# Two transformer blocks in one fp32 kernel: fillers recounted, weights split in halves, and five edits at the seams between stages

## The reference

```python
mixed = einsum('bsgc,gcd->bsgd', pooled - xg, w)
h = mixed.reshape(B, S, D) * scale
...
def _swiglu(x, w_gate, w_up, w_down):
    return (silu(x @ w_gate) * (x @ w_up)) @ w_down
...
def squared_relu_mlp(xn, w_up, w_down):
    return jnp.square(jax.nn.relu(xn @ w_up)) @ w_down
```

## Time and profile before

| what | value |
|---|---|
| time, median of 3 runs | 998.71 us |
| the profiled execution's own time | 998.4 us |
| its span, first to last instruction | 996.2 us |
| TensorE matmul / weight load busy | 977.4 / 863.7 us |
| VectorE / ScalarE / GpSimd busy | 665.5 / 449.8 / 32.4 us |
| mean granted TensorE clock | 0.999 |
| chain that ended last | 88% TensorE |
| bytes moved by DMA | 176.2 MB, 177 GB/s |

### The profile page before, as it was taken

One profiled execution on the slowest core, in us unless ns is written; L12 is line 12 of the kernel. 1 busy time (PEld: TensorE's weight loads), 2 busy tenths in 40 slices (PEclk: granted clock), 3 DMA queues, 4 the chain that ended last, 5 costly groups with the idle time before them and its releaser, 6 DMA issues.

```text
span 996.2 us, 15345 instructions
## 1 busy us (share of the span) xinstructions
PE 977.4 (98%) x6071; PEld 863.7 (87%) x6071; DVE 665.5 (67%) x814; ACT 449.8 (45%) x562; POOL 32.4 (3%) x54
## 2 busy tenths in 40 slices
PE   8999999999999999999999999999999999999997
PEld 7888888888996888888889878899999888888886
DVE  3776767685776876666676477775876656666663
ACT  3444444445665253434334446565654443434342
POOL 1000001000001000000001000000000000000000
PEclk9999999999999999999999999999999999999999
DMA  9756677548532456656543644543565535656541
GB/s 307 233 185 228 190 238 220 193 147 226 157 128 85 148 192 231 206 194 195 184 146 136 193 143 127 158 128 127 170 212 178 194 135 171 207 176 207 170 168 43
DMA packets 142175, 176.20 MB, mean 177 GB/s; under 512 B 7040, under 2 KB 120898, under 8 KB 142126
## 3 DMA queue, kind: packets, MB, share of 16 engines
q1 hardware_dynamic: 139040, 167.07, 52.1%
q0 software_dynamic: 2464, 8.30, 2.8%
q10 hardware_dynamic: 622, 0.14, 0.1%
HBM read 174.40 MB, written 1.09 MB: 176 GB/s over the span
## 4 chain that ended last, share of the span: by engine, by line
PE 88%; DVE 5%; ACT 3%; issue 2%; DMA 1%; ACTq 1%; POOL 0%; DVEq 0%; POOLq 0%; SPq 0%
PE bank L499 87%; DVE w_lo L990 2%; ACT w_hi L982 1%; PE bank L634 1%; PE bank L742 1%; DMA raw<-w_up 1%; DVE arena L1430 1%; DVE x_both L1360 0%; POOL rstd L1885 0%; ACTq L1250 0%; ACT bank L1258 0%; DVE arena L1455 0%; DVE arena L1444 0%; ACT arena L1139 0%; ACTq L1253 0%
## 5 line engine op out<-in xcount | busy, mean ns | idle before, releaser
L990 DVE TENSOR_TENSOR w_lo<-raw,w_hi 128x2048 fp32r<-128x2048 f32 (+1 forms) x157 | 353.5, 2256 | 164.2 <-ACT w_hi L982 164.0
L499 PE MATMUL bank<-x_both,w_hi 128*128 128x256 f32 (+1 forms) x2128 | 439.3, 330 | 2.6 <-DVE arena L1430 1.4
L499 PEld LDWEIGHTS bank<-x_both,w_hi 128*128 128x128 f32 x2128 | 357.6, 189 | 44.3 <-issue 6.7
L982 ACT ACTIVATE w_hi<-raw 128x2048 fp32r<-128x2048 f32 (+1 forms) x157 | 294.9, 1881 | 109.6 <-PE bank L499 98.7
L499 PE MATMUL bank<-x_both,w_lo 128*128 128x256 f32 x1520 | 287.6, 283 | 0.4 <-DVE arena L1430 0.4
L499 PEld LDWEIGHTS bank<-x_both,w_lo 128*128 128x128 f32 x1520 | 230.2, 191 | 3.9 <-issue 0.6
L499 PE MATMUL bank<-w_hi,arena_r 128*128 128x512 f32 x608 | 172.5, 392 | 1.2 <-DVE arena_r L1463 1.0
L499 PEld LDWEIGHTS bank<-w_hi,arena_r 128*128 128x128 f32 x608 | 113.1, 188 | 25.6 <-issue 2.4
L499 PE MATMUL bank<-w_lo,arena_r 128*128 128x512 f32 x304 | 96.1, 391 | 0.0
L1430 DVE TENSOR_REDUCE arena<-bank 128x512 f32<-128x1024 f32 x57 | 69.7, 1222 | 24.8 <-PE bank L499 24.8
L499 PE MATMUL bank<-w_hi,x_both 128*128 128x512 f32 x256 | 75.0, 393 | 2.3 <-DVE x_both L1360 0.8
(11 more groups left out here) (155 smaller groups left out, 612.2 us busy)
## 6 DMA issues: line engine op xcount, KB each, us to landing
raw<-w_up SPq DMA_DIRECT2D x76, 512.0 KB, 4.6
raw<-w_down SPq DMA_DIRECT2D x76, 512.0 KB, 4.3
raw<-w_in SPq DMA_DIRECT2D x60, 512.0 KB, 4.5
raw<-w_gate SPq DMA_DIRECT2D x44, 512.0 KB, 4.8
raw<-w_qkv SPq DMA_DIRECT2D x24, 512.0 KB, 5.0
raw<-w_o SPq DMA_DIRECT2D x16, 512.0 KB, 4.4
table<-bias_vectors POOLq DMA_DIRECT2D x12, 256.0 KB, 4.9
raw<-w_pa SPq DMA_DIRECT2D x4, 512.0 KB, 4.2
```

The lines of the kernel that those rows point to most:

```text
L499: return nc.tensor.matmul(*a, skip_group_check=True, **k)
L982: last = nc.scalar.activation(o, i, ACT.Copy)
L990: last = nc.vector.tensor_tensor(o, i, h.bitcast(F32), ALU.subtract)
```

## The change

Seven edits:

1. **Fillers.** `keep_warm` counts change from 16, 6, 24, 30, 14, 16 to 12, 3, 13, 12, 12, 7 (norm 0, v norm, norm 3, ahead of norm 4, norm 4, norm 5), and the 5 at the end of each seam to 3. The 10 fillers of `warm` ahead of the mixing become 3.
2. **Start.** The 16 opening fillers become four fp32r products of 512 columns. `pool_scale` comes as one row of 4 KB on ScalarE's queue; TensorE spreads it by two products with a column of ones, VectorE copies them to `gb`. ScalarE's table load is drawn ahead by a tiny activation.
3. **Small products** come ahead of the mixing, and wait for all four copies of the pooled x (`pool_copied`) first.
4. **Halves.** ScalarE and VectorE split each unit in two halves of 1024 columns; `hi_done` counts halves.
5. **MLP chunk 1** uses the banks 6 and 7.
6. **Mixer norm.** VectorE multiplies by the gain alone (`with_gain`), ScalarE applies rstd (`scaled`) and raises `n_ready`; ScalarE's rounding of unit `U_QI + 1` goes behind the seam.
7. In the same norm the rests come in the order (0,0), (0,1), (1,0), (1,1), and the first projection waits for `x_ready` 3 and then 4 of the four, where it waited for 2 and 4.

```diff
-            eng.dma_start(gb[:, 2, :], t["pool_scale"].rearrange("a b -> (a b)").partition_broadcast(P))\
-                .then_inc(scale_in, 16)
...
-            keep_warm(bank[4], 5)
+            keep_warm(bank[4], 3)
...
         def pe_mlp(eng):
-            def up(i, unit, slot, final=False):
+            def up(i, unit, slot, final=False, fresh=False):
                 eng.wait_ge(lo_done, unit + 1)
+                if fresh:
+                    project_apart(slot, pair67).then_inc(unit_done, 1)
+                    return
                 eng.wait_ge(up2_read, i)
...
...
         @block.tensor
         def _(eng):
-            for n in range(4 * KT // 2):
-                c = n % 4 * P
-                last = mm(bank[n // 4][:, c:c + P], warm, warm, start=(c == 0), stop=True)
+            for n in range(4):
+                last = mm(bank[n][:, :], opener[:, 0:P], opener, start=True, stop=True)
             last.then_inc(psum_open, 1)
+            eng.wait_ge(set_done, 3)
+            for _ in range(4):
+                mm(bank[6][:, 0:P], warm, warm, start=True, stop=True)
+            eng.wait_ge(scale_in, 16)
+            for h in range(2):
+                mm(bank[4 + h][:, :], ones[0:1, :], scale_row[:, half(h)], start=True, stop=True)\
+                    .then_inc(scale_spread, 1)
+            for _ in range(3):
+                mm(bank[6][:, 0:P], warm, warm, start=True, stop=True)
+            eng.wait_ge(scale_copied, 2)
             eng.wait_ge(pool_m_in, 16)
...
-            for _ in range(10):
+            for _ in range(3):
                 mm(bank[4][:, 0:P], warm, warm, start=True, stop=True)
+            eng.wait_ge(pool_copied, NG)
+            eng.wait_ge(small_in, SMALL)
+            nc.tensor.transpose(bank[7][:, 0:NROWS], prow, ident[0:NROWS, 0:NROWS]).then_inc(pe_start, 1)
+            eng.wait_ge(set_done, 5)
+            mm(bank[7][0:24, 64:448], tab, onehot, start=True, stop=True).then_inc(pe_start, 1)
+            eng.wait_ge(lam_prod, 1)
+            mm(bank[7][:, 448:450], ones, lprod, start=True, stop=True).then_inc(pe_start, 1)
...
-            eng.wait_ge(small_in, SMALL)
-            nc.tensor.transpose(bank[7][:, 0:NROWS], prow, ident[0:NROWS, 0:NROWS]).then_inc(pe_start, 1)
...
             eng.wait_ge(small_read, 4)
-            pe_norm_end(eng, 0, x, 16, 0)
+            pe_norm_end(eng, 0, x, 12, 0)
...
-            pe_norm_end(eng, 3, x, 24, 3)
+            pe_norm_end(eng, 3, x, 13, 3)
             pe_ffn(eng, 1, 3)
-            keep_warm(bank[5], 30)
-            pe_norm_end(eng, 4, nbuf, 14, 4)
+            keep_warm(bank[5], 12)
+            pe_norm_end(eng, 4, nbuf, 12, 4)
...
-            pe_norm_end(eng, 5, nbuf, 16, 6)
+            pe_norm_end(eng, 5, nbuf, 7, 6)
...
         def round_unit(eng, unit, slot, landed, fresh=False, indexer=False):
...
+            for h in range(2):
+                c = slice(h * UW // 2, (h + 1) * UW // 2)
+                nc.scalar.activation(w_hi[slot][:, c], raw[slot][:, c], ACT.Copy).then_inc(hi_done, 1)
...
         def rest_unit(eng, unit, slot, indexer=False):
...
+            for h in range(0 if indexer else 2):
+                eng.wait_ge(hi_done, unit * 2 + (h + 1))
+                c = slice(h * UW // 2, (h + 1) * UW // 2)
+                last = nc.vector.tensor_tensor(w_lo[slot][:, c], raw[slot][:, c], w_hi[slot][:, c].bitcast(F32),
+                                               ALU.subtract)
             last.then_inc(lo_done, 1)
...
             s_ffn(eng, 1)
+            def scaled(i):
+                eng.wait_ge(rstd_ready, 11 + i)
+                for h in range(2):
+                    eng.wait_ge(zg_ready, 2 * i + h + 1)
+                    nc.scalar.activation(nbuf[:, i, half(h)], nbuf[:, i, half(h)], ACT.Identity,
+                                         scale=rstd[:, i:i + 1]).then_inc(n_ready, 1)
             s_rms(eng, 0, (0,))
-            s_split(eng, U_QI + 1)
+            scaled(0)
             s_rms(eng, 0, (1,))
-            s_rounds(eng, 4)
+            s_rounds(eng, 4, (0,))
+            scaled(1)
+            s_rounds(eng, 4, (1,))
+            s_split(eng, U_QI + 1)
...
             v_ffn(eng, 1)
...
+            def with_gain(i, h):
+                V.tensor_tensor(nbuf[:, i, half(h)], x[:, i, half(h)], gb[:, 2, half(h)], ALU.mult)\
+                    .then_inc(zg_ready, 1)
...
-            v_rms_rows(eng, 0, n_rms, 2, False)
...
-            v_rms_rows(eng, 1, n_rms, 2, False)
```

More of the change, by code:

```diff
@@ L313, in build @@
         scale_in = sem("scale_in")
+        scale_spread = sem("scale_spread")
+        scale_copied = sem("scale_copied")
         ln0_in = sem("ln0_in")
@@ L537, in first_apart @@
             whi, wlo = (part(w, unit % SLOTS, KT) for w in (w_hi, w_lo))
-            eng.wait_ge(hi_done, unit + 1)
+            eng.wait_ge(hi_done, 2 * unit + 2)
             for h in range(2):
@@ L705, in pe_mlp @@
                 unit = U_MLP + 1 + 2 * j
-                up(j + 1, unit, unit % SLOTS)
+                up(j + 1, unit, unit % SLOTS, fresh=j == 0)
                 down(j, unit + 1, (unit + 1) % SLOTS)
@@ L980, in round_unit @@
                 eng.wait_ge(unit_done, unit - (SLOTS - 1))
-            for o, i in split_views(slot, indexer)[0]:
-                last = nc.scalar.activation(o, i, ACT.Copy)
-            last.then_inc(hi_done, 1)
-        def rest_unit(eng, unit, slot, indexer=False):
-            eng.wait_ge(hi_done, unit + 1)
-            his, los = split_views(slot, indexer)
-            for (h, _), (o, i) in zip(his, los):
-                last = nc.vector.tensor_tensor(o, i, h.bitcast(F32), ALU.subtract)
+            if indexer:
+                for o, i in split_views(slot, indexer)[0]:
+                    last = nc.scalar.activation(o, i, ACT.Copy)
+                last.then_inc(hi_done, 2)
+                return
+            for h in range(2):
+                c = slice(h * UW // 2, (h + 1) * UW // 2)
+                nc.scalar.activation(w_hi[slot][:, c], raw[slot][:, c], ACT.Copy).then_inc(hi_done, 1)
+        def rest_unit(eng, unit, slot, indexer=False):
+            if indexer:
+                eng.wait_ge(hi_done, 2 * unit + 2)
+                his, los = split_views(slot, indexer)
+                for (h, _), (o, i) in zip(his, los):
+                    last = nc.vector.tensor_tensor(o, i, h.bitcast(F32), ALU.subtract)
+            for h in range(0 if indexer else 2):
[3 more added lines that the diff above has]
+                                               ALU.subtract)
             last.then_inc(lo_done, 1)
@@ L1253, in _ @@
                 eng.dma_start(dst, src).then_inc(small_in, 16)
+            eng.wait_ge(set_done, 4)
+            nc.scalar.activation(nmax[:, 0, 0:1], minus_half[:, :], ACT.Copy)
             eng.wait_ge(psum_open, 1)
@@ L1491, in v_mlp, with square @@
         def v_mlp(eng):
-            def square(i, unit, fresh=False, final=False):
+            def square(i, unit, fresh=False, final=False, b=4):
                 eng.wait_ge(unit_done, unit + 1)
@@ L1512, in v_mlp @@
             low(0)
-            with eng.Fori(0, (NCH2 - 1) // 3 - 1) as i:
+            for j in range(3):
+                unit = U_MLP + 1 + 2 * j
+                v_split(eng, unit + 2)
+                square(j + 1, unit, b=4 if j else 6)
+                v_split(eng, unit + 3)
+                low(j + 1)
+            with eng.Fori(1, (NCH2 - 1) // 3 - 1) as i:
                 for j in range(3):
@@ L1692, in _ @@
             link = Link(eng, v_link)
-            eng.wait_ge(scale_in, 16)
+            for h in range(2):
+                eng.wait_ge(scale_spread, h + 1)
+                V.tensor_copy(gb[:, 2, half(h)], bank[4 + h][:, :]).then_inc(scale_copied, 1)
+            eng.wait_ge(scale_copied, 2)
             for h in range(2):
@@ L1788, in _ @@
             v_rows(eng, link, 0, n, z_ready)
+            eng.wait_ge(z_ready, 1)
+            with_gain(0, 0)
             n = v_statistics(eng, link, 1, ffn_done)
-            n_rms = rms_variance(eng, link, 0, 0)
+            rms_variance(eng, link, 0, 0)
+            eng.wait_ge(z_ready, 2)
+            with_gain(0, 1)
             v_rows(eng, link, 1, n, z_ready)
-            v_rms_rows(eng, 0, n_rms, 2, False)
-            n_rms = rms_variance(eng, link, 0, 1)
+            eng.wait_ge(z_ready, 3)
+            with_gain(1, 0)
+            rms_variance(eng, link, 0, 1)
+            eng.wait_ge(z_ready, 4)
+            with_gain(1, 1)
             v_low(eng, 4, 0, 0)
-            v_rms_rows(eng, 1, n_rms, 2, False)
+            v_low(eng, 4, 0, 1)
             v_low(eng, 4, 1, 0)
-            v_low(eng, 4, 0, 1)
             v_low(eng, 4, 1, 1)
```

30 lines of the change are left out of this document (15 added, 15 removed).

## The result

The changed kernel takes 987.07 us (median of four executions, 984.73 to 988.58), against 998.73 for the kernel before: a ratio of 0.9885, 95% interval 0.9866 to 0.9904. Forecast were 987.4 and a range of 984.8 to 991.6. The total came out; its terms did not all. The profiled execution took 988.04 us, with a span of 985.8.

What follows compares the result with a forecast made beforehand. TensorE, busy 98% of the span, bounds the kernel. Terms 2.1 + 1.5 + 2.8 + 1.2 + 0.6 - 0.4 + 1.5 + 2.0 = 11.3 us off 998.4 give 987.1, median 987.4; range 984.8 to 991.6.

Steps and rivals of the forecast that it cites:

- Start: Up to FFN 0's first product: product at 28.0 instead of 29.64, 2.0 us with the 0.42 wait at 47.01.
- it ends near 7.3 and delays the pooling by 1 us: Start: spreading the pool scale, two 512-column products and two copies of 0.7, ends near 7.3; the 1 us delay is hidden.
- The bound that I had written for the start: Start term: bounds -1.3, with the spreading at half clock, to 3 us.
- the 0.42 of the earlier trace: Wait at 47.01 in the kernel before: halves make chunk 1's up unit early enough that 0.42 us goes.
- The small products' new place: Start: tile 0's transposes no longer stand behind the small products and copies, for which VectorE's first rest waited some 0.4.
- Halves: Weight units split in two: 1.2 us at the FFNs' last chunks, 0.6 at the output matrix, -0.4 in the attentions.
- the longer instructions can land on the path: Attentions: one step already waits for VectorE; two steps of 0.2 taken, -0.4 us, bounds 0 and -3.2.
- The fixed cost: Each halved unit: 0.16 us more on VectorE, 0.2 on ScalarE; rival that it reaches the path: 1014 us, chance 3%.
- Norm 3: Seam at norm 3: thirteen fillers instead of 24 let transposes start at 338.17, product at 340.28: 2.1 us.
- Norm 4: Seam before the mixer: product at 535.5 instead of 538.88, 3.4 us, of which 0.6 belong to halves; 2.8.
- The clock's fall: Rival: gaps at norms 0 and 4 drop the clock, 1.7 us each; two falls 990.8, all seams and start 995.9; 8%.
- The gains behind the start added up to more, not less: Rival that gains don't add, shortened seams meeting the next late thing: 7.5 us remain, 991.2; chance 20%.

Runs made afterwards that it cites:

- the two later kernels with 128 rows: Changed kernel with 128-row spreading into banks 2 and 3, small products in bank 4, behind 8 opening products: 986.38 us; behind 14: 984.61, 985.07 and 985.46.

## Why the prediction was right, and where it wasn't

- **Start**: forecast 1.6 to the first product, measured -2.0 in the profiled execution. The step that failed is "it ends near 7.3 and delays the pooling by 1 us, which hides behind ScalarE's seeds and copies". I had costed the spreading at full clock; it ran at 1.2 GHz, its second copy ended at 9.54, pooling started 3.9 us later than before (10.18 for 6.31), and ScalarE's copies wait for pooling. The bound that I had written for the start, -1.3, was too narrow as well (the term measured -2.0 + 0.4 = -1.6, with the 0.42 of the earlier trace rows): I had counted the price of the two products, not the half clock on pooling behind them. The small products' new place costs nothing there, as forecast, and gives some 0.5 us between the profiles beside the clock's share, where I had counted 0.4. The 0.42 of the earlier trace rows went, but not by the halves, as I had it: it is gone with whole units too.
- **Halves**: forecast 1.2 + 0.6 - 0.4 = 1.4, measured 3.8. The waits that I had counted as gains were right (0.48 twice, 0.59), but two more (0.47, 0.23) lay in stretches that I hadn't read. The step that failed in the attentions is "the longer instructions can land on the path": I took the 0.33 of the earlier trace rows as a sign of losses, and the halves took that wait away. The fixed cost was oversized too: two halves back to back take 2.36 us on VectorE and 2.00 on ScalarE, against 2.29 and 1.91, so 0.07 and 0.09 more a unit instead of 0.16 and 0.2. That is why the engines are busy 676.6 and 467.0 us, not 690 and 480. The Trainium skill (VectorE: DVE Perf Modes, section on the TRN2 errata) says that each small tile pays the fixed cost again. Here the trace agrees for busy time, 0.07 us more a unit, and the cost did not reach the path.

```profile
502.40 2.36 DVE L1015 TENSOR_TENSOR w_lo<-raw,w_hi 128x1024 fp32r<-128x1024 f32 x2 [0.26 <-ACT w_hi L1003]
```

- **Norm 3**: 2.1 forecast. Undoing all fillers costs 2.1 in that stretch, the v norm's among them. Right. **Norm 5**: 1.5, measured 1.6. **MLP chunk 1**: 1.5, measured 1.6. **Norm 4**: with FFN 1's end 3.4, measured 3.44.
- The first stretch gained 4.5, of which halves and fillers explain 3.7. The rest, 0.8, isn't attributed; the 0.42 of the earlier trace rows is part of it. It is gone also with whole units and with the old start, and no run shows which edit took it away.
- **Rivals.** The clock's fall is a real danger that the change escapes at its seams: its longest gap there is 1.00 us, at norm 0, and its windows show 1.00 until 982 us, 2 us behind the last product. (The kernel before, too, shows its only recorded fall there, from about 994 us on.) The experiments show it at norm 0 and at norm 4, the two places that I had named: the rows there took 1.6 and 1.5 us longer, close to the 1.7 I had priced, though at norm 0 only 1.1 of it reached the product. The second lies behind a gap of 2.23 us. At the start it came where I hadn't looked. The gains behind the start added up to more, not less. So the total was right by luck, by two errors that cancel: start 3.6 too high, the rest 2.7 too low. That leaves 10.4 in the profiled executions for 11.3 forecast; between the medians it is 11.7.

The best version measured is the change with the scale by DMA and the old opening: 984.99 us, ratio 0.9869 (0.9851 to 0.9886) to the kernel before, 2.1 us under the changed kernel's median and with a scatter of 0.1 us. Each held against the kernel before that ran beside it, the two save 13.1 and 11.7 us, some 1.5 apart.

## What to carry to other kernels

Work put into TensorE's opening must be costed at either clock, with everything that runs behind it; a DMA that nobody waits for can be cheaper than moving its work to an engine in its cold phase. Count fillers against the row that releases the next real product, and change them together with what makes that row ready: where three things end within a microsecond, removing one shows little, and taking fillers away before the rows come sooner risks the clock. When pricing an edit to a loop that runs all over the kernel, list every wait that ends on that engine, not the ones in the stages already read.

## What the runs showed of the hardware

The granted clock falls from 2.4 to 1.2 GHz, for a few microseconds, and not only behind idle time. Two fp32 products of 512 columns with one row each stood ahead of a fall, while TensorE was never idle, in both profiles in which the clock was surely up when they ran (falls near 10.4 and 11.9); the same two products with 128 rows did not, in three profiles, and the scatter of the runs went from 2.9 to 0.6 us. (In the two later kernels with 128 rows it was 2.2 and 0.9, so the rows aren't the only source of scatter.) The kernels with 128 rows also issue the scale's DMA later, at 1.98 us for 0.76. Three more falls, one profile each, stood behind the small products (33 and 64 rows) with 0.66 and 0.43 us of idle, behind them with 0.90, and behind fillers with 2.23. Other executions of nearly the same rows, the 984.99 kernel's among them, show none, so one profile doesn't clear a kernel of it. The Trainium skill (TensorE: Matmul & The Clock Gate, section "What's actually happening") has the clock follow how busy TensorE has been. In the rows behind the one-row products it fell with TensorE busy throughout, so here the busy time alone doesn't tell it.

Whether the one-row products also put off the late rise near 13 us in the changed kernel, or its new opening did, isn't told apart: the old opening alone gave 986.87 against 987.07, and no run had the new opening with 128 rows. The moment of the rise varies with the old opening too: near 4.5 us in the kernel before, near 7 with the whole start as before, near 8 in the old-opening run. The column of the granted clock reads 1.00 before its first change, so at the start the clock is to be read from the number of records in a microsecond.
